# A fused transformer block on one core: front and experts in one block, embedding rows made inside the experts' stage, routing and first gather re-ordered

## The chip, the core and the metric

The kernel runs on one core of one Trainium2 chip, in one launch. The metric is device microseconds (us) of one execution; lower is better.

## What is computed

One decoder layer on x of 256 rows by 1024, all float32. Cut to what matters here:

```python
mix  = mixing_sublayer(x, ...)                    # projections, sparse attention, conv module, @ w_out
x    = layer_norm(ALPHA * x + mix)                # first norm: x1 below
logits = x @ w_router + b_router                  # (256, 32)
top_vals, top_idx = top_k(logits, 4); gates = softmax(top_vals)
combine = zeros(256, 32).at[rows, top_idx].set(gates)
for e in range(32):                               # w_gate_up[e]: 1024x2048, w_down[e]: 1024x1024
    g, u = split(x @ w_gate_up[e] + b_gate_up[e]); g = min(g, 7); u = clip(u, -7, 7)
    out += combine[:, e:e+1] * (((u + 1) * g * sigmoid(1.702 * g)) @ w_down[e] + b_down[e])
h    = ALPHA * x + out
ple  = sigmoid(h @ w_ple_gate) * (p @ w_ple_proj) # p: (256, 256); p @ w_ple_proj are "the embedding rows"
y    = layer_norm(h + ple)
```

## The kernel before, in words

Every engine has its own hand-written instruction list; semaphores order them. The program has two blocks, one for the front and one for the experts. At a block's end all engines wait for each other.

**Front** (block one). The queue on SP loads 30 weight chunks, listed in `FRONT`, into a ring of 12 slots; the last is `w_pp`, the embedding projection (1 MB). TensorE (PE) does the projections, attention, the conv statistics, then `mix` (L709) in two halves of 128 rows (t = 0, 1). VectorE (DVE) adds the residual in two pieces of 512 columns for each t (L1024) with statistics (L1028), then normalises (L1034 to L1044) to `x1`. ScalarE (ACT) makes the root (`root`, L869). PE turns `x1` (`turn_x1`, L727), ACT copies it out (`turned`, L880), PE multiplies by the router (`route`, L736). Between these stand the four products of the embedding rows, `embed(n)` (L718), and their copies on ACT (`embedded`, L873).

**Routing.** DVE picks the four experts of each row: maximum, index, cast, four compare-and-add steps (L1049 to L1058) give `mask`. PE sums the masks (L755 to L763), so that each row has a place in its expert's list. DVE makes the one-hot `sel` for two experts (`one_hot`, L423); PE gathers their rows of `x1` into `XT` (`gather`, L338, 32 records), ACT copies it (`xt_out`, L461). An expert with over 64 rows takes a branch `two_rounds`; others `one_round`. `wide` holds these flags. `more` lists experts that need still more passes; PE makes it with L769, L775, L776 and DVE copies it (L1101).

**Experts** (block two). 32 experts with six weight loads of 2 MB each (four of `w_gate_up`, two of `w_down`) go through 11 slots: six pairs of ring slots and five in `arena` (`slot_of`). Load n waits until load n - 11 has been read (`pair_read`). The first 11 loads are issued in block one. The last is `early(10)`, which waits on SP behind a write of the embedding rows to HBM (`pple_rows`, L510, 1 MB) and its completion. In a round PE turns the gates (L344), multiplies gate and up (L350, x64), turns the sums (L357, x8), adds the expert before to the totals (`combine`, L370), gathers for the next two (odd experts only), and multiplies down (L350, x32). DVE and ACT make the SwiGLU between L357 and the down product. The 11 loads in hand are what PE can live on while it runs ahead of the DMA.

**End.** `w_pg` (2 loads) follows the experts' loads, then the rows back from `pple_rows` and the second norm's parameters. PE turns h (L1310) and multiplies by `w_pg` (L1319); DVE and ACT finish the second norm in eight pieces.

The block border on SP reads:

```python
sp.wait_ge(pple_out, 4)
sp.dma_start(pple_rows.rearrange("(t p) d -> p t d", p=P), pple).then_inc(pple_saved, 16)
sp.wait_ge(pple_saved, 16)
early(10)
```

Of the kernel before, what the change touches and what calls it, by code (L numbers as in the profile page):

```python
# [8 lines left out]
NT = S // P  # L9
# [10 lines left out]
CAP = 64  # L20
# [6 lines left out]
TAKEN = -3.4e38  # L27

# [18 lines left out]
         + [("out", 256 * j, 256) for j in range(4)] + [("pp", 0, 1024)])  # L47
# [14 lines left out]
EMBED_BANK = (4, 6, 0, 1)  # L62
# [19 lines left out]
def program(nc, x, xT, pT, w_in, bT, bki, b_in, w_oa, w_oc, w_out, dwT, convT, ln1g, ln1b, w_r, b_r,  # L82
            w_gu, bguT, w_dn, b_dn, w_pg, w_pp, ln2g, ln2b, relb, onehot, passes, out, table, pple_rows):
    F32, I32, U32 = mybir.dt.float32, mybir.dt.int32, mybir.dt.uint32
    ALU, ACT, AX = mybir.AluOpType, mybir.ActivationFunctionType, mybir.AxisListType
    ctx = ExitStack()
    with ctx:
# [63 lines left out]
        pple = view(EX + 14336, 2048).rearrange("p (t d) -> p t d", t=NT)  # L151
# [18 lines left out]
        idx8 = view(o + 313, 16).rearrange("p (t h) -> p t h", t=NT)  # L170
        stats = view(o + 329, 24).rearrange("p (t a b) -> p t a b", t=NT, a=2)
# [23 lines left out]
        idxu = sb("idxu", [P, NT, 8], U32)  # L195
# [8 lines left out]
        pple_saved, pple_in = sem("pple_saved"), sem("pple_in")  # L204
# [62 lines left out]
        def w_view(i):  # L267
            what, _, n = FRONT[i]
            kt = {"oa": 4, "oc": 4, "pp": 2}.get(what, KD)
            return wslot(i)[:, 0:kt * n].rearrange("p (k c) -> p k c", k=kt)  # L270

        src = {"in": w_in, "oa": w_oa, "oc": w_oc, "out": w_out, "pp": w_pp}
# [5 lines left out]
        def front_used(i):  # L278
# [10 lines left out]
            if what == "pp":  # L289
                return pple_done, 4  # L290
# [3 lines left out]

        def slot_of(n):
            i = n % ES
            if i >= NS // 2:
                return extra[i - NS // 2]
            i = 2 * ((NF // 2 + i) % (NS // 2))
            return ring[:, i:i + 2, :].rearrange("p a d -> p (a d)")  # L300

# [5 lines left out]
        def load_pair(sp, n, e, c):  # L307
            sp.dma_start(slot_of(n), pair_source(e, c)).then_inc(e_in[n % ES], 16)

        def pair_read(n):  # L310
            e, c = n // CPE, n % CPE
# [6 lines left out]
        NG = NE * CPE  # L318
        NMP = NG + 2
        LN2 = NG - 3  # L320
        pple_t = slot_of(LN2)[:, 0:2 * D].rearrange("p (t d) -> p t d", t=NT)
        lng2, lnb2 = slot_of(LN2)[:, 2 * D:3 * D], slot_of(LN2)[:, 3 * D:4 * D]
        h = slot_of(NG - 1)[:, 0:2 * D].rearrange("p (t d) -> p t d", t=NT)
        hT = slot_of(NG - 1)[:, 2 * D:4 * D].rearrange("p (k t) -> p k t", k=KD)
        x1_rows = x1.rearrange("p t (c m r) -> p t c r m", c=4, r=2)
        h_rows = h.rearrange("p t (c m r) -> p t c r m", c=2, r=4)
# [3 lines left out]

        def gate_bank(t, j):
            return bank[4 * t + j][:, 0:256]

        def gather(pe):

            for k in range(KD):
                for t in range(NT):
                    mm = pe.matmul(bank[4 + k // 4][:, (k % 4) * P:(k % 4 + 1) * P], x1_rows[:, t, k // 2, k % 2, :],  # L338
                                   sel[:, t, :, :], start=(t == 0), stop=(t == NT - 1))
            return mm  # L340
# [116 lines left out]
        def xt_out(a, n):  # L457

            a.wait_ge(gath_done, n)
            for b in range(2):  # L460
                a.activation(XT[:, 4 * b:4 * b + 4, :, :], bank[4 + b][:, :].rearrange("p (k q c) -> p k q c", k=4, q=2),  # L461
                             ACT.Identity).then_inc(xt_half if b == 0 else xt_ready, 1)

        with nc.Block() as block:
            @block.sync
            def _(sp):
# [19 lines left out]
                def into_ring(n):  # L486
                    for i in (NF + 2 * n - NS, NF + 2 * n + 1 - NS):
                        sp.wait_ge(*front_used(i))
                    early(n)
# [64 lines left out]
            def _(pe):  # L554
# [147 lines left out]
                for t in range(NT):  # L702
                    for j in range(4):
                        if t == 0:
                            wait_chunk(pe, 25 + j)
                        for k in range(KD):
                            if t == 0 and j == 0:
                                pe.wait_ge(merged_ready, k + 1)
                            mm = pe.matmul(bank[4 + 2 * t + j // 2][:, (j % 2) * 256:(j % 2) * 256 + 256],  # L709
                                           merged[:, k, t * P:(t + 1) * P], w_view(25 + j)[:, k, :],  # L710
# [3 lines left out]
                def embed(n):  # L714

                    t, j = n // 2, n % 2
                    for k in range(2):
                        mm = pe.matmul(bank[EMBED_BANK[n]][:, :], pT_sb[:, k, t * P:(t + 1) * P],  # L718
                                       w_view(29)[:, k, j * 512:(j + 1) * 512], start=(k == 0), stop=(k == 1))
                    mm.then_inc(pple_done, 1)  # L720

# [19 lines left out]
                turn_x1(0)  # L741
                pe.wait_ge(ple_in, 16)
                wait_chunk(pe, 29)
                pe.wait_ge(var1, 1)
                embed(0)
                route(0)
                turn_x1(1)
                pe.wait_ge(var1, 2)
                embed(1)
                route(1)  # L750
                embed(2)

                pe.wait_ge(mask_ready, 2)
                pe.wait_ge(pple_out, 2)
                pe.matmul(bank[6][:, 0:NE], upper, mask[:, 0, 0:NE], start=True, stop=True)  # L755
                pe.matmul(bank[6][:, NE:2 * NE], upper, mask[:, 1, 0:NE], start=True, stop=False)
                pe.matmul(bank[6][:, NE:2 * NE], ones, mask[:, 0, 0:NE], start=False, stop=True)

                for t in range(NT):
                    pe.matmul(bank[6][0:1, 2 * NE:3 * NE], ones[:, 0:1], mask[:, t, 0:NE], start=(t == 0), stop=(t == NT - 1))  # L760
                for j in range(NMORE):
                    for t in range(NT):
# [3 lines left out]
                embed(3)  # L766
# [3 lines left out]

                pe.wait_ge(sel_ready, 1)
                gather(pe).then_inc(gath_done, 1)

# [3 lines left out]
                          ).then_inc(list_done, 1)  # L777

            @block.scalar
            def _(a):  # L780
# [90 lines left out]
                def embedded(n):  # L871
                    a.wait_ge(pple_done, n + 1)
                    a.activation(pple[:, n // 2, (n % 2) * 512:(n % 2) * 512 + 512], bank[EMBED_BANK[n]][:, :],  # L873
                                 ACT.Identity
                                 ).then_inc(pple_out, 1)

# [7 lines left out]
                root(0)  # L884
                turned(0)
                embedded(0)
                root(1)
                turned(1)
                embedded(1)
                embedded(2)  # L890
                a.wait_ge(rl_shift, 2)
                a.activation(rl[:, :, :], rl[:, :, :], ACT.Exp).then_inc(rl_exp, 1)
                embedded(3)
                xt_out(a, 1)

            @block.vector
            def _(v):
# [123 lines left out]
                for t in range(NT):  # L1021
                    for j in range(2):
                        v.wait_ge(mix_done, (1, 1, 3, 5)[2 * t + j])
                        nc.vector.scalar_tensor_tensor(res[:, t, j * 512:(j + 1) * 512], x_sb[:, t, j * 512:(j + 1) * 512],  # L1024
                                                       ALPHA, bank[4 + 2 * t + j][:, :], ALU.mult, ALU.add
                                                       ).then_inc(v_chain, 1)
                        v.wait_ge(v_chain, c.up())
                        nc.vector.bn_stats(stats[:, t, j, :], res[:, t, j * 512:(j + 1) * 512]).then_inc(v_chain, 1)  # L1028
                        c.up()
                    v.wait_ge(v_chain, c.n)  # L1030
                    nc.vector.bn_aggr(mv[:, t, :], stats[:, t, :, :]).then_inc(var1, 1)
# [550 lines left out]
```

## Time and profile before

| what | value |
|---|---|
| median of 3 runs | 1235.55 us (1234.15 to 1239.02) |
| the profiled execution, its own time | 1235.69 us |
| its span | 1233.9 us |
| mean granted TensorE clock | 0.981 of full |
| PE busy, share of span | 1174.9 us, 95% |
| DVE busy | 292.3 us, 24% |
| ACT busy | 170.5 us, 14% |
| DMA moved | 448.18 MB |

### The profile page before, as it was taken

To read this page: it belongs to the slowest core of one execution; us is meant where nothing else is said; L and a number is where in the kernel's file an instruction comes from. 1 tells how busy PE (TensorE), PEld (TensorE's weight loads), DVE (VectorE), ACT (ScalarE), POOL (GpSimd) and SP (SyncE) were. 2 spreads that over 40 slices of the span, in tenths; PEclk is the share of its full clock that TensorE was granted. 3 is DMA by queue.
4 is the path that set the end of the run, shared out by engine and by line. 5 is a ranking of instruction groups with operands and counts; after the bars stand their busy time and mean duration, and the time that the engine had idled before them with its cause. 6 is when DMAs were issued, how large, how long until landed. Compare 5 with 4: busy or idle time off the path is not lost.

```text
span 1233.9 us, 13833 instructions
## 1 busy us (share of the span) xinstructions
PE 1174.9 (95%) x5694; PEld 593.9 (48%) x5694; DVE 292.3 (24%) x753; ACT 170.5 (14%) x329; POOL 4.4 (0%) x24
## 2 busy tenths in 40 slices
PE   7999999969999999999997989999999999999987
PEld 5887888843434434343444324344343434434346
DVE  0505944331111311111130111212111121211125
ACT  1213122021101111110110101111110111111012
POOL 0000000000000000000000000000000000000000
PEclk9899999989999999999997989999999999999999
DMA  9962466559999999999999979999999999999990
GB/s 314 349 201 69 138 237 221 201 191 391 427 428 428 426 428 426 428 426 428 429 425 426 426 271 406 430 427 429 426 429 428 427 428 428 426 428 426 429 394 36
DMA packets 63225, 448.18 MB, mean 363 GB/s; under 512 B 6984, under 2 KB 33904, under 8 KB 38320
## 3 DMA queue, kind: packets, MB, share of 16 engines
q1 hardware_dynamic: 58896, 442.94, 87.6%
q10 hardware_dynamic: 4256, 4.24, 1.0%
q8 instruction: 50, 0.82, 0.3%
q14 instruction: 23, 0.19, 0.0%
HBM read 445.05 MB, written 2.11 MB: 362 GB/s over the span
## 4 chain that ended last, share of the span: by engine, by line
PE 67%; DVE 4%; DMA 4%; issue 2%; ACT 1%; DVEq 0%; ACTq 0%
PE bank L350 54%; PE bank L338 5%; DMA ring<-in_w_gu 4%; PE bank L370 3%; PE bank L1319 2%; PE bank L357 2%; DVE arena L396 1%; DVE arena L390 1%; PE bank L344 1%; ACT arena L1372 1%; DVE arena L414 1%; DVE arena L410 1%; PE bank L1251 1%; DVE arena L406 0%; PE bank L1310 0%
## 5 line engine op out<-in xcount | busy, mean ns | idle before, releaser
L350 PE MATMUL bank<-ring,arena 128*64 128x512 f32 x1744 | 387.8, 599 | 14.0 <-DVE arena L396 5.3
L350 PE MATMUL bank<-arena 128*64 128x512 f32 x1424 | 315.5, 596 | 5.3 <-DVE arena L396 4.4
L350 PEld LDWEIGHTS bank<-ring,arena 128*64 128x64 f32 x1744 | 122.7, 138 | 257.4 <-issue 235.2
L350 PEld LDWEIGHTS bank<-arena 128*64 128x64 f32 x1424 | 99.6, 137 | 203.7 <-issue 187.5
L390 DVE TENSOR_TENSOR arena<-bank,arena 128x512 f32<-128x512 f32 x33 | 22.8, 691 | 625.1 <-PE bank L357 625.1
L570 PE MATMUL bank<-arena,ring 128*128 128x256 f32 x576 | 130.3, 388 | 7.8 <-DMA ring<-in_w_in 7.8
L570 PEld LDWEIGHTS bank<-arena,ring 128*128 128x128 f32 x576 | 111.6, 195 | 24.1 <-issue 8.6
L1372 ACT ACTIVATE arena<-bank 128x512 f32<-128x512 f32 x62 | 37.0, 597 | 398.1 <-PE bank L350 398.1
L370 PE MATMUL bank<-arena 64*128 64x512 f32 x272 | 67.6, 615 | 1.4 <-ACT arena L1375 1.4
L338 PEld LDWEIGHTS bank<-arena 128*128 128x128 f32 x512 | 61.5, 196 | 11.4 <-issue 11.4
L338 PE MATMUL bank<-arena 128*128 128x128 f32 x512 | 64.6, 285 | 0.0
L1375 ACT ACTIVATE arena<-bank 128x512 f32<-128x512 f32 x33 | 19.7, 597 | 245.9 <-PE bank L350 243.8
L357 PEld LDWEIGHTS bank<-arena 128*128 128x128 f32 x264 | 36.7, 209 | 34.9 <-issue 25.9
L357 PE MATMUL bank<-arena 128*128 128x128 f32 x264 | 48.8, 309 | 3.0 <-ACT arena L1372 0.4
L969 DVE SCALAR_TENSOR_TENSOR arena<-arena 128x256 f32<-128x256 f32 x120 | 48.3, 479 | 0.0
L370 PEld LDWEIGHTS bank<-arena 64*128 64x128 f32 x272 | 23.4, 186 | 23.8 <-issue 16.8
L803 ACT ACTIVATE arena<-bank,arena 128x256 f32<-128x256 f32 x36 | 16.9, 472 | 127.7 <-PE bank L570 127.7
L423 DVE TENSOR_TENSOR arena<-arena 128x256 f32<-128x256 f32 x16 | 6.8, 425 | 105.0 <-PE bank L344 105.0
L414 DVE TENSOR_TENSOR arena<-arena 128x256 f32<-128x256 f32 x66 | 28.1, 425 | 5.3 <-ACT arena L419 0.9
L410 DVE SCALAR_TENSOR_TENSOR arena<-arena 128x256 f32<-128x256 f32 x66 | 28.0, 425 | 4.1
L695 PE MATMUL bank<-arena,ring 128*128 128x256 f32 x128 | 27.8, 379 | 0.0
L709 PE MATMUL bank<-ring,arena 128*128 128x256 f32 x128 | 27.8, 379 | 0.0
(195 smaller groups left out, 550.6 us busy)
## 6 DMA issues: line engine op xcount, KB each, us to landing
ring<-in_w_gu SPq DMA_DIRECT2D x71, 2048.0 KB, 26.0
arena<-in_w_gu SPq DMA_DIRECT2D x57, 2048.0 KB, 26.3
ring<-in_w_dn SPq DMA_DIRECT2D x36, 2048.0 KB, 25.2
arena<-in_w_dn SPq DMA_DIRECT2D x28, 2048.0 KB, 25.1
ring<-in_w_in SPq DMA_DIRECT2D x19, 1024.0 KB, 13.3
ring<-in_w_out SPq DMA_DIRECT2D x4, 1024.0 KB, 5.8
ring<-in_w_oa SPq DMA_DIRECT2D x2, 1024.0 KB, 4.9
ring<-in_w_oc SPq DMA_DIRECT2D x2, 1024.0 KB, 5.0
```

The costliest lines, as they stand in the source:

```text
L338: mm = pe.matmul(bank[4 + k // 4][:, (k % 4) * P:(k % 4 + 1) * P], x1_rows[:, t, k // 2, k % 2, :], sel[:, t, :, :], start=(t == 0), stop= ...
L350: mm = pe.matmul(to[half * CAP:(half + 1) * CAP, :], rows, w[:, half * 512:(half + 1) * 512], start=first, stop=last)
L357: mm = pe.transpose(to[:, j * P:(j + 1) * P], blocks[:, j, :], ident)
L370: mm = pe.matmul(total[t][n][:, :], G2[a:a + CAP, q, t * P:(t + 1) * P], ysb[a:a + CAP, :], start=first, stop=last)
L390: nc.vector.tensor_tensor(by_bias(gt, 8), by_bias(of_gate[:, :], 8), bias_of(e, 0, 0, 8), ALU.add).then_inc(sw_step, 1)
L410: nc.vector.scalar_tensor_tensor(up[:, at], up[:, at], 1.0, gt[:, at], ALU.add, ALU.mult).then_inc(sw_step, 1 + 6 * skip * j)
L414: nc.vector.tensor_tensor(to[:, at], up[:, at], sg[:, at], ALU.mult).then_inc(act_ready, 1 + 2 * skip * j)
L570: mm = pe.matmul(bank[n % 4][:, 0:S], w[:, k, j * P:(j + 1) * P], xT_sb[:, k, :], start=(k == 0), stop=(k == KD - 1))
L695: mm = pe.matmul(bank[n % 4][:, 0:S], w_view(i)[:, k, (c % 4) * P:(c % 4 + 1) * P], rhs[:, k, :], start=(k == 0), stop=(k == 3))
L709: mm = pe.matmul(bank[4 + 2 * t + j // 2][:, (j % 2) * 256:(j % 2) * 256 + 256], merged[:, k, t * P:(t + 1) * P], w_view(25 + j)[:, k, :], ...
L969: nc.vector.scalar_tensor_tensor(cy[:, a, :], u_sb[:, a, bass.ds(j, S)], dw[:, a, bass.ds(j, 1)], cy[:, a, :], ALU.mult, ALU.add).then_inc ...
L1372: a.activation(rows, of[:, :], ACT.Identity).then_inc(h_out, 1 + 2 * j)
```

## The change

What it does, part by part:

1. **One block.** The two blocks become one; no engine waits for all others between front and experts. `read_flag` now waits for `more_out` (DVE's copy of the list) before the flag of expert 1, and for `wide_ready` before the first flag.
2. **Embedding rows.** `w_pp` leaves `FRONT` and becomes load 168 (`PP`) of the experts' stage, before the first load of expert 28. It takes one of the 11 slots; the rows stay in it, so the loads behind it share 10. `embed` runs on PE in expert 28 (t = 0) and in expert 30 (t = 1), four 128x512 products each, before the down product. ACT copies them out. The write to and read from `pple_rows` are gone.
3. **SP.** `into_ring(5)` and `early(10)` follow directly on the other early loads, ahead of the biases `b_dn`.
4. **Routing.** DVE takes max, a memset of places 4 to 7, match-replace and one comparison instead of index, cast and four steps. `cum_done` is signalled once after the two row sums, again after the counts. The counts go to bank 4.
5. **First gather.** It uses banks 0 and 1 and stands before L769's product; each half signals, and ACT copies each half when it is there.
6. **Bias turn.** The two transposes of `gate_rows` move from the start of block two into expert 0, behind its turned sums.
7. **Residual.** Four pieces of 256 columns for each t; t = 1 uses one bank for each piece, so piece j can start when its product is done.

The diff, cut to its core (moved lines left out):

```diff
-         + [("out", 256 * j, 256) for j in range(4)] + [("pp", 0, 1024)])
+         + [("out", 256 * j, 256) for j in range(4)]
+        PP_E = NE - 4
+        PP = PP_E * CPE
+        NG = NE * CPE + 1
...
+            if n != PP:
+                slots.append(i)
...
-                into_ring(5)
-                sp.wait_ge(pple_out, 4)
-                sp.dma_start(pple_rows.rearrange("(t p) d -> p t d", p=P), pple).then_inc(pple_saved, 16)
-                sp.wait_ge(pple_saved, 16)
-                early(10)
+                into_ring(5)
+                early(10)
+                sp.wait_ge(zeroed, 2)
+                for n in range(2):
+                    sp.dma_start(ysb[n * CAP:n * CAP + NE, :], b_dn[:, n * 512:(n + 1) * 512]).then_inc(bias_rows, 16)
+                for n in range(ES, NG):
+                    sp.wait_ge(*pair_read(last_in[n]))
+                    if n == PP:
+                        sp.dma_start(wpp, w_pp.rearrange("(k p) d -> p k d", p=P)).then_inc(e_in[slot_no[n]], 16)
...
-                nc.vector.max_index(idxu[:, t, :], top8[:, t, :], rl[:, t, :]).then_inc(v_chain, 1)
-                nc.vector.tensor_copy(idx8[:, t, :], idxu[:, t, :]).then_inc(v_chain, 1)
-                for r in range(TOPE):
-                    nc.vector.scalar_tensor_tensor(mask[:, t, 0:NE], iota_e, idx8[:, t, r:r + 1],
-                                                   mask[:, t, 0:NE], ALU.is_equal, ALU.add)
+                nc.vector.memset(top8[:, t, TOPE:8], NOT_THERE).then_inc(v_chain, 1)
+                nc.vector.match_replace(picked[:, t, :], top8[:, t, :], rl[:, t, :], TAKEN).then_inc(v_chain, 1)
+                nc.vector.tensor_scalar(mask[:, t, 0:NE], picked[:, t, :], TAKEN, None, ALU.is_equal
+                                        ).then_inc(mask_ready, 1)
...
+                def embed(e):
+                    t = (e - PP_E) // 2
+                    if t == 0:
+                        pe.wait_ge(ple_in, 16)
+                        pair(PP)
+                    for j, to in enumerate((gate_sum, up_sum)):
+                        for k in range(2):
+                            mm = pe.matmul(to[:, :], pT_sb[:, k, t * P:(t + 1) * P], wpp[:, k, j * 512:(j + 1) * 512],
+                                           start=(k == 0), stop=(k == 1))
+                        mm.then_inc(pple_done, 1)
...
+                    if e == 0:
+                        turn_bias(gate_sum)
                     before(e)
                     if q == 1 and e < NE - 1:
                         next_gather(e)
+                    if e in (PP_E, PP_E + 2):
+                        embed(e)
                     use_down(e, weights)
```

How the lists stand against each other on PE, from the last products of the router to the block border. Before (L736 is `route` of t = 1, L718 `embed`, L755 to L763 the sums, L338 the gather, L769 to L776 the list of further passes, L464 the border):

```order
L736 MATMUL bank<-wr_sb,arena 128x32 x8
L718 MATMUL bank<-ring,arena 128x512 x2
L755 MATMUL bank<-arena 128x32
L756 MATMUL bank<-arena 128x32
L757 MATMUL bank<-arena 128x32
L760 MATMUL bank<-arena 1x32 x2
L763 MATMUL bank<-arena 32x1 x4
L718 MATMUL bank<-ring,arena 128x512 x2
L769 MATMUL bank<-arena 64x1
L338 MATMUL bank<-arena 128x128 x16
L775 MATMUL bank<-arena 1x16
L776 MATMUL bank<-arena 1x1
```

After (L784 is `route`, L794 to L802 the sums, L356 the gather, L810 to L813 the list, L489 the flag's read, which belongs to expert 0):

```order
L784 MATMUL bank<-wr_sb,arena 128x32 x8
L794 MATMUL bank<-arena 128x32
L795 MATMUL bank<-arena 128x32
L796 MATMUL bank<-arena 128x32
L799 MATMUL bank<-arena 1x32 x2
L802 MATMUL bank<-arena 32x1 x4
L356 MATMUL bank<-arena 128x128 x16
L810 MATMUL bank<-arena 64x1
L812 MATMUL bank<-arena 1x16
L813 MATMUL bank<-arena 1x1
L489 TENSOR_LOAD wide
```

The embedding products have left this stretch, L810 stands behind the gather, and no branch to another block comes after the list.

PE in expert 28 of the change (L389 is `combine`, L917 the embedding products, L369 the down product):

```order
L363 MATMUL bank<-arena 128x128 x2
L369 MATMUL bank<-ring,arena 64x512 x16
L369 MATMUL bank<-arena 64x512 x16
L376 MATMUL bank<-arena 128x128 x8
L489 TENSOR_LOAD wide
L389 MATMUL bank<-arena 128x512 x4
L917 MATMUL bank<-ring,arena 128x512 x4
L369 MATMUL bank<-arena 64x512 x16
```

The products stand where PE otherwise waits for the SwiGLU. Expert 30 reads alike.

## Rows read from the trace of the kernel before

**Rows 1.** Windows: PE, PEld, DVE, ACT, POOL busy us, then clock, DMA share, GB/s.
```profile
700.00:725.00 25.00, 18.24 (x84) 7.55 (x82) 8.15 (x20) 3.92 (x7) 0.00 (x0) 0.86 0.73 294
...
1150.00:1175.00 25.00, 22.22 (x104) 7.56 (x102) 4.08 (x10) 2.70 (x5) 0.00 (x0) 1.00 1.01 427
```

**Rows 2.** Waits of PE: what waited for what, us in total, times, longest.
```profile
PE bank L1286 <- PEq L464: 8.1, 1, 8.1
...
PE bank L344 <- issue: 7.5, 2, 5.5
...
PE bank L350 <- DMA ring<-in_w_gu: 3.4, 3, 1.2
```

**Rows 3.** Chain that ended last: start, us, what (expert 0, then expert 2).
```profile
276.23 15.62 PE bank L350 x64
...
332.83 13.88 PE bank L350 x64
```

**Rows 4.** Timeline of the border stretch: start, us, engine, line [idle before <-releaser].
```profile
247.48 0.69 DVE L1024 SCALAR_TENSOR_TENSOR arena<-arena,bank 128x512 f32<-128x512 f32 x1 [5.49 <-PE bank L709]
...
248.93 0.21 DVE L1031 BATCH_NORM_AGGREGATE arena<-arena 128x2 f32<-128x12 f32 x1
...
250.89 0.16 DVE L1037 RECIPROCAL arena<-arena 128x1 f32<-128x1 f32 x1 [0.95 <-ACT arena L869]
...
253.34 0.66 PE L727 MATMUL bank<-arena 128*128 128x128 f32 x4 [0.79 <-DVE arena L1044]
...
253.84 1.88 PE L718 MATMUL bank<-ring,arena 128*128 128x512 f32 x4
...
254.04 0.60 ACT L880 ACTIVATE arena<-bank 128x512 f32<-128x512 f32 x1 [0.85 <-PE bank L727]
...
255.56 1.87 PE L736 MATMUL bank<-wr_sb,arena 128*128 128x32 f32 x16
...
257.46 0.19 DVE L1049 TENSOR_TENSOR arena<-bank,arena 128x32 f32<-128x32 f32 x1 [2.01 <-PE bank L736]
...
258.42 1.11 DVE L1058 SCALAR_TENSOR_TENSOR arena<-arena 128x32 f32<-128x32 f32 x4
...
259.59 0.41 PE L755 MATMUL bank<-arena 128*128 128x32 f32 x2 [0.37 <-DVE arena L1058]
...
260.38 0.28 PE L760 MATMUL bank<-arena 128*1 128x32 f32 x4
...
261.21 0.43 DVE L423 TENSOR_TENSOR arena<-arena 128x256 f32<-128x256 f32 x1
...
262.83 4.04 PE L338 MATMUL bank<-arena 128*128 128x128 f32 x32
...
266.85 0.18 PE L776 MATMUL bank<-arena 64*1 64x1 f32 x2
...
273.77 0.33 SPq L308 DMA_DIRECT2D arena<-in_w_dn  x1
...
275.15 0.66 PE L1286 MATMUL bank<-arena 128*128 128x128 f32 x2 [8.11 <-PEq L464]
...
296.72 7.09 PE L350 MATMUL bank<-ring,arena 128*64 128x512 f32 x32 [1.43 <-DVE arena L396]
```

**Rows 5.** Timeline of PE in experts 30 and 31.
```profile
1157.03 7.09 PE L350 MATMUL bank<-arena 128*64 128x512 f32 x32 [0.56 <-DVE arena L396]
...
1178.76 3.65 PE L350 MATMUL bank<-ring,arena 128*64 128x512 f32 x16 [1.24 <-DMA ring<-in_w_gu]
```

**Rows 6.** Window of 1 us, PE alone: busy, clock, DMA share, GB/s.
```profile
30.00:31.00 1.00, 1.00 (x10) 0.77 1.10 348
```

**Rows 7.** Window of the routing stretch, all engines; columns as in rows 1.
```profile
248.00:257.00 9.00, 8.05 (x49) 5.80 (x47) 6.07 (x18) 3.58 (x7) 0.77 (x2) 1.00 0.35 147
```

**Rows 8.** Timeline of PE: narrow matmuls at the start, gather of the two-round expert.
```profile
27.96 4.68 PE L592 MATMUL bank<-ring,arena 128*128 128x8 f32 x32
...
664.96 7.09 PE L1251 MATMUL bank<-arena 128*128 128x64 f32 x32 [0.38 <-DVE arena L445]
```

More of the change, by code:

```diff
@@ L27 @@
 TAKEN = -3.4e38
+NOT_THERE = 3.4e38
 NMORE = (S - WIDE) // CAP
@@ new lines, in rows_of, with next_gather, before @@
+                def rows_of(e, q, last=False, done=None):
+                    pe.wait_ge(rows_out, e * 2 + 2)
+                    combine(pe, q, last=last, done=done)
+                def next_gather(e):
+                    pe.wait_ge(sel_ready, e // 2 + 2)
+                    gather(pe)
+                def before(e):
+                    if e == 0:
+                        pe.wait_ge(bias_rows, 32)
+                        pe.wait_ge(bias_ready, 1)
+                        combine(pe, 1, first=True)
+                    else:
+                        rows_of(e - 1, 1 - e % 2)
@@ new lines, in _, with weights @@
+                pe.br("pe_end")
+                for e in range(NE):
+                    nc.switch_bb(f"pe_two_rounds{e}", parent=top)
+                    two_rounds(e)
+                    pe.br(f"pe_rounds_done{e}")
+                nc.switch_bb("pe_more", parent=top)
+                n_more = pe.value_load(more[0:1, LIST:LIST + 1], min_val=0, max_val=LIST)
+                rows_of(NE - 1, 1)
+                with pe.Fori(0, n_more) as r:
+                    e = r + NE
+                    def weights(c):
+                        n = NMP + c
+                        pe.wait_ge(e_in[slot_no[n]], r * 16 + filled[n])
+                        return slot_of(n)
+                    pe.wait_ge(sel_ready, r + (NE // 2 + 1))
+                    gather(pe)
+                    pe.wait_ge(selg_ready, r + (NE // 2 + 1))
+                    turn_gates(pe, selg[:, 0]).then_inc(sgt_done, 3)
+                    pe.wait_ge(xt_ready, r + (NE // 2 + 1))
+                    use_gate_up(e, 0, weights)
+                    for j, (rows, to) in enumerate(((h_gate, gate_turned), (h_up, up_turned))):
+                        pe.wait_ge(h_out, e * 4 + (1 + j))
+                        if j:
+                            pe.wait_ge(g2_out, e * 3 + 3)
+                        turn(pe, rows, to).then_inc(t_done, 1 + 2 * j)
+                    use_down(e, weights)
+                    rows_of(e, 0)
@@ L779, in _ @@
+                for t in range(NT):
+                    for n in range(2):
+                        pe.matmul(total[t][n][:, :], ident, gate[:, 0, NE:NE + 1].to_broadcast([P, 512]),
+                                  start=False, stop=True).then_inc(comb_done, 1)
+                pe.br("pe_last")
+                nc.switch_bb("pe_end", parent=top)
             @block.scalar
@@ L894, in _, with gates_out, sums_out @@
-                xt_out(a, 1)
+                xt_out(a, 1, 0)
+                top = nc.cur_bb
+                flag = a.alloc_register("act_two_rounds")
+                def gates_out(e, q, of, to, skip):
+                    a.wait_ge(sgt_done, e * 3 + to)
+                    a.activation(G2[:, q, :], of[:, 0:S], ACT.Identity).then_inc(g2_out, 1 + skip)
+                def sums_out(e):
+                    for j, (rows, of) in enumerate(((h_gate, gate_sum), (h_up, up_sum))):
+                        a.wait_ge(gu_done, e * 2 + (1 + j))
+                        a.activation(rows, of[:, :], ACT.Identity).then_inc(h_out, 1 + 2 * j)
@@ new lines, in _ @@
+                a.wait_ge(wide_ready, 2)
+                read_flag(a, flag, 0)
+                a.br("act_experts")
+                for e in range(NE):
+                    nc.switch_bb(f"act_two_rounds{e}", parent=top)
+                    two_rounds(e)
+                    a.br(f"act_rounds_done{e}")
+                nc.switch_bb("act_more", parent=top)
+                n_more = a.value_load(more[0:1, LIST:LIST + 1], min_val=0, max_val=LIST)
+                with a.Fori(0, n_more) as r:
+                    e = r + NE
+                    xt_out(a, r + (NE // 2 + 1))
+                    gates_out(e, 0, up_turned, 3, 2)
+                    sums_out(e)
+                    sigmoid(a, e, 0, False)
+                    a.wait_ge(d_done, e * 2 + 2)
+                    rows_from(gate_turned, 2)
```

740 lines of the change are left out of this document (334 added, 406 removed).

## The prediction

> **What bounds the kernel now.** I read the windows first, then the waits of TensorE (PE), then the chain that ended last, then the timeline of the border and of the end. In the experts' stage PE is busy nearly all the time and the DMA moves 427 GB/s [rows 1]. Both are near their limit, and they take turns. One load of 2 MB is 2.097 MB / 427 GB/s = 4.9 us, so six loads of an expert are 29.5 us. PE gets through an expert in some 27 us: 332.83 less 276.23 is 56.6 for two experts [rows 3], of which 1.7 are the slow clock of the first (below) and 0.9 its longer wait for DVE, 1.43 against 0.56 [rows 4, 5]. PE therefore eats into the 11 loads in hand. The two-round expert near 700 us refills them: the DMA is down to 0.73 of its share there, because all slots are full [rows 1]. From then on PE lives on the stock until experts 30 and 31, where it waits for the DMA 3.4 us in all [rows 2], the last time 1.24 us before the load at 1178.76 [rows 5]. The consequence: whatever the front gives is kept in full, since the stock is full again after the two-round expert and both clocks of the stage start from there. What is added to the DMA in the last four experts is paid.
>
> At the border PE stands idle for 8.1 us [rows 2]. The chain is visible in the timeline: PE ends the list at 267.0, SP issues its last early load at 273.77, behind a write of the embedding rows and its completion, and only then do the engines meet; PE works again at 275.15 [rows 4]. Expert 0's gate and up then take 15.62 us instead of 13.88 [rows 3], as PE begins them at 1.2 GHz.
>
> **The change, part by part**, as seen in PE's start of expert 0 (before: 276.2).
>
> *Residual in pieces.* The last piece starts at 247.48 as before. Step and statistics of 512 columns take until 248.93 [rows 4]; a DVE step of 256 columns is 0.43 (L423), so two take 0.9: about 0.5 earlier, with an aggregate over four pieces a little longer. For t = 0 all pieces come at once and cost some 0.5 us more on DVE, hidden behind the mix of t = 1 on PE. If that cover went, it would cost that 0.5.
>
> *Root.* DVE waits 0.95 us for the reciprocal's input [rows 4], because ACT copies embedding rows ahead of it. That copy is gone: 0.95. The second half of x1 is ready 1.4 us earlier.
>
> *Router of t = 1.* From the turning of that half at 253.34 to the end of L736 at 257.43 are 4.1 us, since PE first does an embedding product at 253.84 [rows 4]. Without it: 0.66 to turn, 0.60 for ACT's copy, half of L736's 1.87, two hand-overs, about 2.4. Gain 1.7; sum 3.1.
>
> *Mask.* L1049's start to L1058's end is 2.07 us [rows 4]. In its place stand an add, a maximum, a memset, a match-replace of two instructions and a comparison, on 32 columns or fewer. DVE's steps of that size are 0.19 (L1049) to 0.28 (a quarter of L1058). The trace has no memset on DVE and no match-replace so narrow: five to six steps by these bounds are 0.95 to 1.7; I take 1.2, nearest to L1049's size. Gain 0.9; sum 4.0.
>
> *Sums and one-hot.* From L755 to the one-hot at 261.21 are 1.62. DVE no longer waits for L760 and the counts (0.4) nor does the threshold first (0.2). Gain 0.6. The gather began 1.2 us after the one-hot ended, behind an embedding product and L769 [rows 4]; now nothing stands there: gain 1.1; sum 5.7. The gather would begin at 257.1.
>
> *Gather and list.* L338 is 4.04; behind it come L769, DVE's step, and the list, in series now: 0.9 against 0.2. Loss 0.8; sum 4.9; the list ends at 262.1.
>
> *Border.* From the list's end to L1286 are 8.1, then the bias turn of 0.5 before the round. A flag read and a branch remain; bounds are 0.1 and 1.4 (273.77 + 0.33 to 275.15, which holds them and the meeting). I take 0.6. Gain 8.1; sum 13.0. Expert 0 would multiply at 263.2. ACT and DVE still jump to the experts' code, now beside PE's 14 us of gate and up. SP loses nothing: its loads come 11 to 20 us earlier, and the biases, now behind two loads, are needed only at the first combine, 14 us later.
>
> *Clock of expert 0.* If PE enters it at 2.4 GHz, 15.62 less 13.88 is 1.7 more. Sum 14.7.
>
> *Bias turn in expert 0.* Two transposes, an ACT copy and the table load behind it now stand ahead of the sigmoid. DVE's wait had PE idle for 1.43 before the down product [rows 4]; it grows by the copy and ACT's flag read: 0.4 to 1.5, I take 0.9. Sum 13.8.
>
> *Clock in the routing.* Before, the clock stayed at 1.00 from 248 to 257, with PE busy 8.05 of 9 [rows 7]; there wide embedding products stood between the 32-column products of the router. They are gone, and from about 252.5 to 257 PE has only L736, three sums and counts. The nearest row is the start: PE was busy 1.00 in the microsecond at 30, inside narrow matmuls that began at 27.96, and yet the clock went from 1.00 to 0.50 [rows 6, 8]. I take it that it falls here too, before the gather. A gather of 32 records at half clock took 7.09 [rows 8] against 4.04, so 3.05 if it is slow throughout; in expert 0 the clock came back within some 3.5 us of dense work (1.74 lost), so the low end is 1.5. I take 2.3. Sum 11.5.
>
> Rules of the Trainium skill, "TensorE: Matmul & The Clock Gate". Its section "Why this matters for your kernels" ties throughput drops to idle gaps between bursts of matmuls; by it the clock stays, since the longest gap left is near 1.2 us, and the result is the first rival. The row at 30 us speaks against it as the whole rule. The section "Part 4: PE-mode transpose" says that transposes do not count as PE work in the same way; by it the clock would fall sooner, the second rival.
>
> *Embedding products in experts 28 and 30.* Two products (four records) cost PE 1.72, from 253.84 to 255.56, so four cost 3.44. Of this 0.56 hides in PE's wait before the down product [rows 5]: 2.9 an expert, 5.8 in all. ACT's two copies (0.6 each) lie beside the down product. Against it stands the 3.4 us wait for the DMA, which these products use up: PE would be 2.4 later. *The load.* 1.05 MB at 427 GB/s is 2.5 us more before the last loads, all of which PE waits for. PE takes the later of the two, 2.5. *The slot.* Ten instead of eleven are nothing while the stock is nearly empty: every free slot is refilled at once and some eight loads are queued. The transfers to and from `pple_rows` gone save nothing more: the read came after everything PE needs. Sum 9.0.
>
> **Sum.** 1235.7 (the profiled execution, 0.1 above the median) less 9.0 is 1226.7; I forecast **1226.6**.
>
> **The rivals.**
> 1. *The clock is kept* through routing and gather: 2.3 more, 1224.3. For it: 248 to 257 stayed at 1.00 though PE had gaps. 0.30.
> 2. *The clock falls early and stays low into expert 0*: 3.05 for the gather and 1.74 as before: 13.8 - 3.05 - 1.74 - 2.5 = 6.5 gained, 1229.2. 0.12.
> 3. *The embedding products are not hidden* by the DMA wait: 5.8 + 2.5 = 8.3 instead of 2.5, so 1232.5. It would take a stock empty before expert 28; the first wait in the rows is later. 0.05.
> 4. *The border does not go as it says*: PE fetches expert 0's code cold. In front of the two-round code PE had one such wait of 5.5 [rows 2]. With the forecast's clock 1232. Against it: the new code follows in line. 0.06.
> 5. *The slot* (other side). If loads are limited by the way from free slot to landing rather than by bandwidth, ten slots stretch each of the last 26 loads by a tenth of 4.9 us: 12.7 + 2.5 against 11.5 gained, so 1239. It decides from the point at which DMA share falls under 1.0 with PE waiting; it was 1.01 at 1150 [rows 1]. 0.03.
>
> The forecast has 0.44. **Range:** 1223.0 to 1231.5; it takes in rivals 1 and 2 and a microsecond or two for the mask, the flag read and the bias turn. A measurement of this kernel can tell about 0.5% (6.2 us) from no change, so faster means under 1229.4: the forecast, rival 1 and three quarters of rival 2, 0.83. The same: the rest of rival 2, rivals 3 and 4, 0.14. Slower (over 1241.7): rival 5 with the clock of rival 2 on top, 1239 + 2.6, 0.03.
>
> **What would show it.** PE's idle before expert 0 under 2 us, and its L350 (now L369) starting at 263 to 266. The mask chain near 1.2 us; the gather starting within 0.1 us of the one-hot. The clock column at 0.50 in 256 to 262 for the forecast, 1.00 for rival 1. In expert 30 the DMA at 1.0 and PE's waits on it under 3 us; rival 3 shows waits and products side by side, rival 5 a DMA share under 1.0 after load 168. I am wrong if the experts' stage from 15 on shifts by anything but what the front gave.

## The result and the profile after

The changed kernel takes 1220.49 us (median of four runs, 1219.16 to 1221.01) against 1235.3 us before. The ratio is 0.9873, 95% interval 0.9851 to 0.9896: 14.8 us less, where 9.1 were forecast. That is 1.3%, clear of the noise. The time lies under the forecast range of 1223.0 to 1231.5. Medians here and below are of all executions, while ratios and their intervals leave out three executions at a lower granted clock, of 1273.3, 2022.9 and 2037.3 us. The profiled execution has a span of 1219.0 us against 1233.9.

The border stretch in the timeline of the kernel after (start us, us, engine, line, shapes, and in brackets the idle time before and what ended it):

```profile
247.24 0.42 DVE L1413 SCALAR_TENSOR_TENSOR arena<-arena,bank 128x256 f32<-128x256 f32 x1 [2.57 <-PE bank L766]
...
251.58 0.66 PE L775 MATMUL bank<-arena 128*128 128x128 f32 x4 [0.80 <-DVE arena L1432]
...
252.07 2.83 PE L784 MATMUL bank<-wr_sb,arena 128*128 128x32 f32 x16
...
254.94 0.19 DVE L1437 TENSOR_TENSOR arena<-bank,arena 128x32 f32<-128x32 f32 x1 [2.31 <-PE bank L784]
...
256.05 0.64 PE L794 MATMUL bank<-arena 128*128 128x32 f32 x2 [1.14 <-DVE arena L1445]
...
257.90 0.42 DVE L442 TENSOR_TENSOR arena<-arena 128x256 f32<-128x256 f32 x1
...
258.38 6.09 PE L356 MATMUL bank<-arena 128*128 128x128 f32 x32 [0.35 <-DVE arena L442]
...
265.17 0.18 PE L813 MATMUL bank<-arena 64*1 64x1 f32 x2
...
265.84 0.43 PE L363 MATMUL bank<-arena 128*128 128x128 f32 x2 [0.48 <-issue]
266.20 13.95 PE L369 MATMUL bank<-ring,arena 128*64 128x512 f32 x64
...
285.15 7.09 PE L369 MATMUL bank<-ring,arena 128*64 128x512 f32 x32 [0.72 <-DVE arena L415]
```

These answer to [rows 4]. The 8.1 us at the border are 0.48. The gather follows the one-hot at once, but takes 6.09 us instead of 4.04. The last row is expert 0's down product: 285.15 against 296.72, so 11.6 us are won up to there.

The clock behind the slow gather, in windows of 1 us of PE alone (busy, clock, DMA share, GB/s):

```profile
251.00:252.00 1.00, 0.42 (x4) 1.00 0.99 426
252.00:253.00 1.00, 1.00 (x11) 0.88 1.03 442
253.00:254.00 1.00, 1.00 (x6) 0.50 1.03 442
...
262.00:263.00 1.00, 1.00 (x6) 0.50 0.00 0
263.00:264.00 1.00, 1.00 (x11) 1.00 0.00 0
```

It fell to 1.2 GHz inside the router's 32-column products and came back before expert 0, in the last quarter of the gather.

The waits of PE, which answer to [rows 2]:

```profile
PE bank L363 <- issue: 2.2, 2, 1.7
...
PE bank L369 <- DMA ring<-in_w_gu: 0.5, 1, 0.5
```

PE waits for the DMA 0.5 us instead of 3.4. And the waits marked "issue" ahead of the turned gates, 7.5 us before, are 2.2, and 0.48 of that stands in front of expert 0. (A further wait marked "issue", 5.3 us at the end of the two-round expert, is the same in every run.) Nothing in the forecast touched this. Where does it lie? The chain that ended last, before, around the entry of the two-round expert (start, us, what):

```profile
656.36 2.02 issue
658.38 0.33 PE bank L344
658.71 5.50 issue
664.21 0.39 PE bank L344
```

And after:

```profile
644.79 1.72 issue
646.51 0.45 PE bank L363 x2
...
647.33 6.02 PE bank L962 x32
```

| PE starts | before | after | won so far |
|---|---|---|---|
| expert 1 (gates turned) | 303.73 | 292.17 | 11.6 |
| expert 15 | 731.51 | 714.29 | 17.2 |
| last `combine` | 1194.24 | 1179.30 | 14.9 |

So the front gave 11.6, expert 14 another 5.7, and the last four experts took 2.3 back: from expert 15 to expert 28 the two kernels take the same 352.8 us.

### The profile page after: what moved, and what is told of

It reads as the page before. It is cut to its first block, busy times and chain, and to the rows that moved or that the text cites. A ratio compares the mean times of both kernels' runs of the same rounds, so it can differ in the third digit from the quotient of the medians.

```text
span 1219.0 us, 13824 instructions
## 1 busy us (share of the span) xinstructions
PE 1176.4 (97%) x5694; PEld 596.6 (49%) x5694; DVE 291.2 (24%) x755; ACT 172.3 (14%) x329; POOL 4.4 (0%) x24
## 4 chain that ended last, share of the span: by engine, by line
PE 88%; DVE 4%; DMA 4%; ACT 1%; issue 1%; SPq 0%; DVEq 0%; ACTq 0%
PE bank L369 55%; PE bank L627 10%; PE bank L356 5%; DMA ring<-in_w_gu 3%; PE bank L389 3%; PE bank L1028 2%; PE bank L766 2%; PE bank L752 2%; PE bank L376 2%; PE bank L676 1%; DVE arena L415 1%; PE bank L363 1%; DVE arena L409 1%; ACT arena L1187 1%; DMA ring<-in_w_in 1%
## 5 line engine op out<-in xcount | busy, mean ns | idle before, releaser
L369 PE MATMUL bank<-ring,arena 128*64 128x512 f32 x1712 | 379.2, 597 | 9.9 <-issue 5.3
L369 PE MATMUL bank<-arena 128*64 128x512 f32 x1456 | 323.2, 598 | 4.6 <-DVE arena L415 3.9
L369 PEld LDWEIGHTS bank<-ring,arena 128*64 128x64 f32 x1712 | 120.6, 137 | 246.6 <-issue 231.7
L369 PEld LDWEIGHTS bank<-arena 128*64 128x64 f32 x1456 | 102.2, 138 | 208.0 <-issue 194.2
L627 PE MATMUL bank<-arena,ring 128*128 128x256 f32 x576 | 131.0, 389 | 7.4 <-DMA ring<-in_w_in 7.4
L1187 ACT ACTIVATE arena<-bank 128x512 f32<-128x512 f32 x62 | 37.1, 598 | 396.1 <-PE bank L369 396.1
L389 PE MATMUL bank<-arena 64*128 64x512 f32 x272 | 67.6, 615 | 2.0 <-ACT arena L1190 1.4
L356 PEld LDWEIGHTS bank<-arena 128*128 128x128 f32 x512 | 63.6, 202 | 11.8 <-issue 11.4
L356 PE MATMUL bank<-arena 128*128 128x128 f32 x512 | 66.6, 290 | 0.3 <-DVE arena L442 0.3
L1190 ACT ACTIVATE arena<-bank 128x512 f32<-128x512 f32 x33 | 19.7, 597 | 249.6 <-PE bank L369 247.5
L376 PEld LDWEIGHTS bank<-arena 128*128 128x128 f32 x264 | 36.7, 209 | 34.9 <-issue 25.9
L376 PE MATMUL bank<-arena 128*128 128x128 f32 x264 | 48.8, 309 | 2.9 <-ACT arena L1187 0.4
L389 PEld LDWEIGHTS bank<-arena 64*128 64x128 f32 x272 | 23.5, 186 | 24.4 <-issue 17.6
L480 ACT ACTIVATE arena<-bank 128x512 f32<-128x512 f32 x32 | 19.1, 597 | 70.2 <-PE bank L356 70.2
L1028 PE MATMUL bank<-arena 128*128 128x256 f32 x128 | 27.8, 379 | 0.0
```

The costliest lines, as they stand in the source:

```text
L356: mm = pe.matmul(bank[b + k // 4][:, (k % 4) * P:(k % 4 + 1) * P], x1_rows[:, t, k // 2, k % 2, :], sel[:, t, :, :], start=(t == 0), stop= ...
L369: mm = pe.matmul(to[half * CAP:(half + 1) * CAP, :], rows, w[:, half * 512:(half + 1) * 512], start=first, stop=last)
L376: mm = pe.transpose(to[:, j * P:(j + 1) * P], blocks[:, j, :], ident)
L389: mm = pe.matmul(total[t][n][:, :], G2[a:a + CAP, q, t * P:(t + 1) * P], ysb[a:a + CAP, :], start=first, stop=last)
L627: mm = pe.matmul(bank[n % 4][:, 0:S], w[:, k, j * P:(j + 1) * P], xT_sb[:, k, :], start=(k == 0), stop=(k == KD - 1))
L1028: mm = pe.matmul(gate_bank(t, j), hT[:, k, t * P:(t + 1) * P], pg_view(k, j), start=(k == 0), stop=(k == KD - 1))
```

## Experiments

Each difference is against the kernel before or the change, measured beside the run. The front itself differs between executions of one kernel: the change began its gather at 258.4 in one trace and 261.0 in another. To keep that out I also read the *stage time*, from the start of expert 1 to the last `combine`. It is 890.5 us in both traces of the kernel before and 887.1 in both of the change.

*before_again*: the kernel before, unchanged.

> The kernel before, unchanged. Placement theory (PE's wait at the entry of the two-round expert is set by where its code lies): the same two waits as in the trace of before, near 2.0 and 5.5 us, a single transpose between them. Rival (the wait is set by the DMA traffic of that moment): the waits differ by over 1 us from the first trace.

1235.25 us, ratio to before 0.9993 (0.9975 to 1.0012). The two waits are 1.86 and 5.50 us, again with one transpose between. They are a fixture of this program, not of the moment.

*before_shift4*: code that never runs grows by two transposes.

```diff
                 def two_rounds(e):
                     q = e % 2
+                    if e == 0:
+                        for _ in range(1):
+                            turn_gates(pe, selg[:, q])
```

> The kernel before with two transposes more (four machine instructions) in the two-round code of expert 0, which is never run; so the two-round code of expert 14 lies four instructions further on, as it does in the change. Placement theory: one wait of 1.7 to 2.0 us, none of 5.5 us, time down by 5.5 us, about 1229.8 us. Rival (one block, or the traffic of the moment): no change, 1235.3 us.

1228.33 us against 1236.78, ratio 0.9923 (0.9894 to 0.9952). Its chain:

```profile
656.10 2.24 issue
658.34 0.67 PE bank L344 x2
```

The 5.5 us are gone, and nothing that is executed was changed. The waits fall by 5.3 us (7.5 to 2.2), the stage time by 4.1 (890.5 to 886.4). The difference is not lost at the end: from expert 15 to the last `combine` it takes 462.4 us, before 462.7, and its waits for loads are the same 3.4. It is lost inside expert 14, where the half clock behind the entry now lies on more of PE's work (L350 x128 takes 30.10 us there against 29.11). The medians differ by more than the waits, 8.4 us and 6.9 against *before_again*; the trace is of the slowest of the four executions, 1231.29.

*after_shift252* and *after_shift128*: the same with 63 and 32 calls of `turn_gates` in the change.

```diff
+                    if e == 0:
+                        for _ in range(63):
+                            turn_gates(pe, selg[:, q])
```

> The changed kernel with 126 transposes more (252 machine instructions) in the never-run two-round code of expert 0, so that the code of expert 14 lies, counted in stretches of 256, where it lay before. Placement theory with stretches of 256: two waits again, 2 and 5.5 us, time up by about 5.5 us, 1226.0 us. Rival: no change, 1220.5 us.

> The changed kernel with 64 transposes more (128 machine instructions) there, the control of the run before: code in the middle of a stretch. Placement theory: one wait of 1.7 to 2.0 us, time 1220.5 us within 0.7. Rival that any shift disturbs it: slower.

252 instructions: 1226.76 us, ratio to before 0.9915 (0.9883 to 0.9946). 128: 1218.91, ratio 0.986 (0.9832 to 0.9887). The chain with 252:

```profile
644.59 7.92 issue
652.51 0.60 PE bank L363 x2
```

and the wait with 128:

```profile
PE bank L363 <- issue: 1.9, 1, 1.9
```

A shift that is 256 in sum (4 and 252) brings the long wait back. It is one wait of 7.9 us now, with no transpose between, where I expected two, so the place is not exactly that of the kernel before. A shift by 128 brings no long wait. The stage times are 894.8 and 885.4.

The traces hold a more direct proof, which needs no counting. Their DMA records have a queue q8, marked "instruction", with packets of 16,384 bytes. Around the entry of expert 14 they read (us from the span's start):

| run | place of the code against before | first packet | second packet | PE's waits end at |
|---|---|---|---|---|
| before | 0 | 655.85 to 656.96 | 661.76 to 662.85 | 658.38 and 664.21 |
| before_shift4 | +4 | 655.81 to 656.91 | 661.92 to 663.00 | 658.34 |
| the change | +4 | 643.98 to 645.08 | 650.14 to 651.24 | 646.51 |
| after_shift128 | +132 | 643.94 to 645.04 | 649.80 to 650.88 | 646.45 |
| after_shift252 | +256 | 644.16 to 645.26 | 649.96 to 651.05 | 652.51 |
| after_no_products (below) | -12 | 647.12 to 648.21 | 653.56 to 654.58 | 649.66 and 656.04 |

In all the traces every one of these waits ends 1.3 to 1.5 us after a packet has landed: the short one after the first, the long one after the second, which starts 5.8 to 6.4 us behind the first. The second packet comes in every run; PE waits for it only where it needs it early. So PE waits for its instructions there. Two kernels and five places show this.

The run with 128 cannot tell a unit of 256 from one of 128, as +4 and +132 are the same place counted by 128. The number of packets can: the kernel before has 50 for 11,388 recorded instructions of PE, matmuls and weight loads, 228 for each, so a packet holds more than 128. With the return of the long wait at +256 this makes 256 by far the likeliest unit.

**Was it SP's write that held the border?** *before_no_write* leaves out the write of the embedding rows; at the end x is read in their place.

```diff
-                sp.dma_start(pple_rows.rearrange("(t p) d -> p t d", p=P), pple).then_inc(pple_saved, 16)
-                sp.wait_ge(pple_saved, 16)
...
-                sp.dma_start(pple_t, pple_rows.rearrange("(t p) d -> p t d", p=P)).then_inc(pple_in, 16)
+                sp.dma_start(pple_t, x.rearrange("(t p) d -> p t d", p=P)).then_inc(pple_in, 16)
```

> The kernel before without the write of the embedding rows to HBM and SP's wait for it; at the end x is read in their place, a transfer of the same size. Theory (the border lasts as long as SP's queue does): the last early load is issued at 263 instead of 273.8, PE's idle at the border falls from 8.1 to about 1 us, the clock stays at 2.4 GHz into expert 0, and the time falls by 8 to 9 us to 1227. Rival (the meeting of the engines itself costs it): idle stays over 6 us, time down by less than 2 us.

1227.57 us against 1235.8, ratio 0.9935 (0.9912 to 0.9959): 8.2 us less. Of this 6.3 are the border; in this trace the gather also began 1.8 us sooner than in that of the kernel before (261.06 against 262.83).

```profile
261.59 0.35 SPq L308 DMA_DIRECT2D arena<-in_w_dn  x1
...
267.12 0.41 PE L1284 MATMUL bank<-arena 128*128 128x128 f32 x2 [1.85 <-PEq L464]
...
267.77 15.59 PE L350 MATMUL bank<-ring,arena 128*64 128x512 f32 x64
```

The idle time falls from 8.1 to 1.85: the meeting of the engines is cheap, what it waited for was not. One part of what I expected fell: the clock was not kept, and expert 0's products still take 15.6 us. The clock fell here although the stop was only 1.85 us long, and was 0.84 in the microsecond from 267 and 0.50 in the next.

**What do the embedding products and their load cost in the last experts?** *after_no_products* makes each product 8 columns wide.

```diff
-                        for k in range(2):
-                            mm = pe.matmul(to[:, :], pT_sb[:, k, t * P:(t + 1) * P], wpp[:, k, j * 512:(j + 1) * 512],
-                                           start=(k == 0), stop=(k == 1))
+                        mm = pe.matmul(to[:, 0:8], pT_sb[:, 0, t * P:(t + 1) * P], wpp[:, 0, 0:8],
+                                       start=True, stop=True)
```

> The changed kernel with each 128x512 embedding product replaced by one of 8 columns; the load of w_pp stays. Theory (PE takes the later of its own work and the DMA; the products stand in what was a wait for the DMA): PE's wait for the last expert's loads grows from 0.5 to about 6 us and the time stays at 1220.5 within 0.7. Rival (the products are paid in full): 5.8 us less, 1214.7.

It was slower than the change: 1228.51 us, ratio to before 0.9927 (0.9899 to 0.9955), where both theories said equal or faster. *after_no_embed* also loads 8 columns of `w_pp` only.

> The same, and of w_pp only 8 columns are loaded, so that the 1 MB is gone too. Theory: the last loads arrive 2.5 us earlier and PE waits for them: 1218.0 us. Rival (products paid in full, load free): 1214.7 us. Rival (neither counts): 1220.5 us.

1222.71 us. Neither number is an answer, for I had moved the code of expert 14 by 16 instructions without wanting to. The chain of after_no_products:

```profile
647.42 2.24 issue
649.66 0.45 PE bank L363 x2
...
650.49 0.68 PE bank L961 x4
651.17 4.87 issue
656.04 6.04 PE bank L961 x28
```

The target now lies 16 instructions further forward, 12 ahead of its place in the kernel before, and PE gets through two transposes and four gather records before it runs dry: 12 instructions by my count, and some waits between. *after_no_embed* shows the same two waits, 1.66 and 4.61 us. This is what a leave-out experiment does when code position counts. I repeated both with four calls of `turn_gates` in never-run code to put the 16 instructions back.

*after_again* is the change once more as their base.

> The changed kernel, unchanged, as the base for the others of this call: 1220.5 us within 1; PE's wait at the entry of the two-round expert 1.7 to 2.2 us in one piece.

1221.91 us (1220.57 to 1222.99), stage time 887.1, wait at the entry 2.0 us.

*after_no_products_placed*:

> As after_no_products (each embedding product one of 8 columns, w_pp still loaded), but with 16 machine instructions put back into never-run code, so that the two-round code of expert 14 lies where it lies in the change. Placement theory: the wait of 4.9 us at its entry is gone. With it, PE takes the later of its own work and the DMA: time as after_again within 0.7, PE's waits for the last loads near 5 us. Rival (products paid in full): 5.8 us less.

1219.76 us. The long wait at expert 14 is gone. The median is 2.1 us under after_again, which is neither of the two forecasts; but the gather of its trace began 3.6 us earlier, and the stage time is 886.9 against 887.1. The waits for loads show why:

```profile
PE bank L369 <- DMA ring<-in_w_gu: 5.1, 5, 1.3
...
PE bank L369 <- DMA arena<-in_w_gu: 0.5, 1, 0.5
```

They grew from 0.6 to 5.6 us. Expert 28 takes 25.32 us without the products and 28.33 with them, so the two experts are some 6 us shorter without them, and the waits take up most of that. The products cost nothing; they fill time in which PE would wait for the DMA.

*after_no_embed_placed*:

> As after_no_embed (8 columns of w_pp loaded, 1 MB less), placed in the same way: 2.5 us less than after_again, with waits for the last loads near 3.5 us. Rival (load free): the same as after_no_products_placed.

1218.76 us, 3.1 less than after_again, but only 1.0 less than *after_no_products_placed*, and these two ranges overlap (1218.51 to 1220.78 and 1218.99 to 1221.46). The stage time is 884.9, 2.2 less than in the change; yet *after_shift128*, which has nothing to do with the load, moved it by 1.8. The stretch from expert 15 to the last `combine` leaves out both the front and the two-round expert, and it decides:

| embedding in the last experts | traces | from expert 15 to the last `combine` |
|---|---|---|
| none (the kernel before twice, *before_shift4*, *before_no_write*) | 4 | 462.4 to 462.7 us |
| load and products (the change twice, both shifts, both with fill) | 6 | 465.0 to 465.3 us |
| load, products of 8 columns | 2 | 465.0 and 465.2 us |
| 8 columns loaded, products of 8 columns | 2 | 462.7 and 463.0 us |

The load is what costs, 2.2 us.

**Can the clock be kept?** *after_fill* adds two wide products into bank 4 which nobody reads.

```diff
+                def fill():
+                    pe.matmul(bank[4][:, :], ident, x1[:, 0, 0:512], start=True, stop=True)
...
+                        if t == 1 and k == 4:
+                            fill()
...
                     route(t)
+                fill()
```

> The changed kernel with two additional 128x512 products whose result nobody uses, in PE's waits of the routing: one between the halves of the turning of t = 1, one before the sums of the masks. Theory (the clock falls there because only narrow matmuls are left): the clock stays at 2.4 GHz through the gather, the gather takes 4.0 instead of 6.1 us, the sums and the router 1 us less, the two products cost up to 1 us: 1218.5 us. Rival (PE's gaps alone bring the clock down, or two products are too few): no change or up to 1 us slower.

1217.14 us, ratio to before 0.9858 (0.9832 to 0.9883).

```profile
252.04 1.93 PE L789 MATMUL bank<-wr_sb,arena 128*128 128x32 f32 x16
253.80 1.11 PE L771 MATMUL bank<-arena 128*128 128x512 f32 x2
...
256.81 4.04 PE L356 MATMUL bank<-arena 128*128 128x128 f32 x32 [0.50 <-DVE arena L442]
...
262.57 13.95 PE L369 MATMUL bank<-ring,arena 128*64 128x512 f32 x64
```

Router, gather and expert 0 all run at full speed; expert 0 begins 3.6 us earlier than in the change. In windows of 1 us of PE alone:

```profile
252.00:253.00 1.00, 1.00 (x11) 1.00 0.88 377
253.00:254.00 1.00, 1.00 (x10) 1.00 1.11 475
...
256.00:257.00 1.00, 0.50 (x13) 1.00 1.15 492
```

The DMA was as busy here as in the change, so its traffic did not bring the clock down. *after_fill_again* is the same beside the change on one chip.

> after_fill once more, beside the change on the same chip: two unused wide products in the routing keep the clock. Expected 3.0 us less than after_again (expert 0 began 3.6 us earlier in its first trace). If the clock is a matter of chance from run to run, the difference is under 1 us.

1217.35 us (1216.60 to 1217.42) against 1221.91 for the change: 4.6 us less, with ranges that do not meet, and ratio 0.9855 (0.9838 to 0.9871) to the kernel before. Its gather took 4.04 us again. This version beats both kernels. Its stage time is 887.4, so all of the gain is ahead of expert 1. The two products account for 3.6 us of it: from the turning of x1's first half to expert 0 are 15.6 us in both traces with them and 19.2 in both without. What makes up the rest of the 4.6 is not shown; ahead of that point the front differs from one execution to the next.

In all eight traces of the change and its variants without the two products the clock fell between 249 and 256 us, in both with them it did not. What about them keeps it is not shown: they are wide, and they also fill PE's waits of 0.8 and 1.1 us.

## Why the prediction was wrong, point by point

**The border and the front, 11.5 forecast, 11.6 measured.**
- Residual and root: from the last piece's start to the second turn of x1 4.3 us against 5.9 [rows 4]. Forecast 1.4 less, measured 1.5.
- Router of t = 1: from 251.58 to 254.90 are 3.3 against a forecast 2.4; the 0.9 are the clock, which fell one step earlier than I put it (L784 2.83 us, with the clock kept 1.93).
- Mask: 254.94 to 255.99, 1.05 us; I took 1.2.
- Sums to one-hot: 1.85 instead of 1.0, at half clock; in *after_fill*, at full clock, 1.2. Gather behind the one-hot at once, as forecast.
- Gather 6.1, most of it at half clock, 2.0 over the fast one; with router and sums 3.6 went to the clock, as *after_fill* gives back, where I took 2.3. That is the size that was off.
- Border: 0.5 us from list to gates; I took 0.6. With the turn of the gates expert 0 begins 0.85 us behind the list; I took 1.1. Expert 0 at full clock, as forecast.
- Bias turn: L376 to the down product 5.1 us, before 4.9: 0.14 more where I took 0.9. This 0.8, with the border, the mask and a last residual piece that began 0.24 sooner than before, paid for the clock's excess. That 11.5 met 11.6 so closely is luck in part.

**The end, 2.5 forecast, 2.3 measured**, and the runs say for the forecast's reason: the products are free, the load costs 2.2. PE takes the later of its own work and the DMA.

**What failed: the step that was not there.** The sum treated the experts' stage from 1 to 27 as unchanged ("whatever the front gives is kept in full"). I had the 5.5 us wait among my rows, but used it only as the price of rival 4, for the code of expert 0, and never asked whether the change moves the code in front of which it stood. It did, by four instructions by my count, and expert 14 became 5.7 us shorter, more than a third of the whole gain. In its place the runs show a wait for PE's second packet of instructions, 5.5 us before and gone in the change. The same four instructions in the kernel before shorten expert 14 by 3.8; the other 1.9 are mostly the clock behind the entry, at 0.50 for 17.1 us before, 13.7 in *before_shift4* and 10.2 in the change, where the gather takes 6.02 us instead of 7.09. The forecast's own sign of being wrong, a stage from expert 15 on that shifts by something else than the front gave, is what happened: 17.2 against 11.6 at the start of expert 15.

With the long wait brought back by a shift of 252, the change measures 10.0 us less than the kernel before beside it (1226.76 and 1236.78), where 9.1 were forecast; with the long wait absent from both, 9.4 less (1218.91 in *after_shift128*, 1228.33 in *before_shift4*). So the mechanisms of the forecast account for 9 to 10 us, and the accident of placement for the rest. The sum is no proof of each term, as the clock and the bias turn erred in opposite directions.

Of the rivals, 1 (clock kept) fell for the change and is what after_fill makes true; 2 was half right, the clock fell early but was back for expert 0; 3 is refuted by after_no_products_placed; 4 by the 0.48 us in front of expert 0, though its kind of wait, for code not yet there, was what decided at expert 14; 5 by a stage that lost 2.3 us and no more. The rule of the Trainium skill, "TensorE: Matmul & The Clock Gate", section "Why this matters for your kernels", ties the fall to gaps between bursts of matmuls: here PE's longest gap from 246 us to the fall was 0.8 us, and in the trace shown the clock fell with narrow products running. The kernel before had a gap of 0.79 us at the same step and kept the clock [rows 4, 7]; it made the same transposes too, with wide products between. So the measurement decides against gaps alone. At 30 us the clock fell with PE busy throughout, in narrow products [rows 6, 8], which speaks for the width of the work; that width alone decides is not shown.

## What to carry to other kernels

Read waits marked "issue" behind rarely taken branches, and hold them against the packets of the instruction queue. Where a wait ends shortly after a packet has landed, it depends on where code lies, any edit ahead of it can add or remove several microseconds, and an experiment that leaves instructions out must put their number back into code that never runs, or it measures the move.

A stretch of narrow matmuls with short waits in front of dense work can cost the clock; here two wide products that nobody needs, placed in waits that existed anyway, gave back 3.6 us. And where two resources take turns at the limit, price an addition by the later of the two and not by their sum: 6 us of products were free here, 1 MB was not. To measure such a term, choose a stretch that leaves out what varies: the medians here could not separate 2.2 us from the front's own spread, the stretch from expert 15 on could.

## What was not expected of the hardware

- A branch of PE to new code waited 1.7 to 2.2 us, and 4.6 to 5.8 us more where the target lay shortly ahead of a border that in these runs came back after 256 instructions; once it was one wait of 7.9. The waits ended 1.3 to 1.5 us after packets of the instruction queue had landed, and the second packet started 5.8 to 6.4 us behind the first.
- Two unused 128x512 products (1.0 to 1.1 us each) kept 2.4 GHz through 12 us of small work, worth 3.6 us in the traces and 4.6 between the medians.
- The meeting of all engines at a block's border took 1.85 us of PE's time when no engine was late.
